# Turning 128 x 128 blocks in one run instead of one by one between other products, and new begin times for every lane of the plan

## The chip, the cores and the metric

The kernel runs on one core of a Trainium2 chip. The metric is the device time of one execution in microseconds (us), from the first to the last instruction and a little around them; the times stand below. A core has four engines that matter here: TensorE (PE, with PEld for its weight loads), VectorE (DVE), ScalarE (ACT) and GpSimd (POOL), and SyncE (SP), which here only issues the transfers.

## The reference, cut to what matters

Two models of two layers each run one after the other on 256 tokens of width 1024, all in float32.

```
for l in range(2):                                     # first model
    h += 0.5 * swiglu(rmsnorm(h), gate, up, down)      # ffn1, width 2816
    z = rmsnorm(h) @ w_in                              # mix1: latent attention (8 heads),
    h += (sum of 3 gated branches) @ w_out             #   differential attention (8 heads), pooling
    h += 0.5 * swiglu(...)                             # ffn2
h = rmsnorm(h)                                         # final
for l in range(2):                                     # second model
    x += 0.5 * rmsnorm(swiglu(rmsnorm(x)))             # ffn1_2
    x += rmsnorm(token_mixing(rmsnorm(x)))             # mix2: windowed attention, mLSTM, RWKV-7
    x += 0.5 * rmsnorm(swiglu(...))                    # ffn2_2
    x += rmsnorm(sigmoid(rmsnorm(x) @ w_gate) * (p[l] @ w_proj))   # ple
```

## The kernel before, in words

The 256 tokens are two tiles (i = 0, 1) of 128 rows. A stage is a part of a layer (`ffn1`, `mix1`, `ffn2`, `final`, `ffn1_2`, `mix2`, `ffn2_2`, `ple`); `s` counts them. The weights come from memory as one stream of pieces of 512 KB. ACT rounds each to fp32r (`whi`, L471), DVE makes the rest (`wlo`, L478), and each product of the reference is three products in fp32r (`products`, all recorded at L489): whi with the activation's high part, wlo with the high part, whi with the low part. They are called dense products here; nearly all have 512 columns.

Everything else on PE is small and in float32. There are the turns (transposes, `turns`, L498), which bring activations into the layout that the next dense products need: the normed rows (`pe_norm`, names `xs`), the hidden layer of an FFN (`pe_hidden`, names `hid`, four turns in each of 11 steps `q`), the attention weights (`pe_values1`, `pe_values2`, names `S`), the projections (`pe_chunks`), the attention outputs (`pe_turn`). Then the scores (L1411, L1420, L2401), the products with the values (L1456, L2424), the 64 x 64 products of the RWKV part (`quad`, L2050, and L2094 to L2180), and the small products of the mLSTM part (L2516 to L2553).

The order of the instructions of each engine is fixed when the program is made. Each piece of work is a generator, a lane (`pe_ffn`, `act_norm`, `dve_jobs1`, ...). A lane yields a beat, a planned time, ahead of its next instructions; `by_beat` always takes the lane with the lowest beat. A beat is only a key to sort by: on the chip, an engine runs its list in order and waits on semaphores. `timed` replaces the beats of a lane by those of the table `PLAN` for the two stages that meet (`org(s)` plus the entry); a tuple that a lane yields, as `(t + MM * q,)`, is a beat relative to its last begin time, with `MM = 0.227`. So a lane that yields such a tuple between two instructions lets other lanes put theirs in between:

```
    def gemm(...):   # dense: one beat for each product
                if q:
                    yield (t + MM * q,)
                m = pe.do.matmul(...)
    def turns(t, *each):   # turns: one beat for each
            if q:
                yield (t + MM * q,)
            m = pe.do.transpose(o, src, ident)
```

The pieces of weights are placed on ACT and DVE by `round_beat`, from the beats at which PE takes a piece and frees its slot.

Of the kernel before, what the change touches and what calls it, by code (L numbers as in the profile page):

```python
# [88 lines left out]
def by_beat(*lanes):  # L89
# [6 lines left out]
    while heads:  # L96
# [5 lines left out]
        else:  # L102
# [6 lines left out]
MM = 0.227  # L109
# [3 lines left out]
        "act_norm": (-10.4, 2.5, 2.72, 21.46),  # L113
        "act_square": (-68.48, -48, 17.2, 28.38),
        "dve_norm": (-87.72, -87.72, -70, 30.08),
        "dve_square": (16.08, 24.78),
        "pe_norm": (-171.14, -161.94, -122.64, -103.54),
        "pool_norm": (-115.96, -48.5),
    },
    "ffn1>mix1": {  # L120
        "act_back1": (72.74, 77.9, 95.8, 107.48, 125.74, 125.74, 128.12, 130.52, 135.62, 139.32, 139.4, 143.98, 148,
            158.54, 162.44, 165.88, 165.88, 168.4, 174.62, 178.06),
        "act_bias1": (-33.68,),
        "act_branch1": (128.68, 130.56, 138.26, 143.04, 160.14, 161.8, 174.62, 178.68, 187.66, 187.7, 208.74,
            208.74),
        "act_jobs1": (56.56, 66.82, 66.82, 69.38, 70.48, 81.86, 94.32, 94.32, 94.32, 99.16, 117.22, 126.44, 129,
            131.22, 131.46, 136.5, 137.28, 141.96, 146.98, 148.52, 164.4, 164.74, 168.26, 172.98),
        "act_latent": (29.56, 30.88, 31.94, 38.5, 41.42, 42.62, 42.62, 44.34, 46.06, 46.84, 49.64, 51.5, 51.94),
        "act_merged1": (199.54, 202.84, 212.96, 214.02),
        "act_norm": (16.38, 19.78, 23.28, 27.08),  # L130
        "act_pool1": (111.82, 120.26, 125.26, 145.8),
        "act_project1": (41.96, 63.54, 80.82, 105.12),
        "act_square": (23.3, 24.76, 25.46, 25.46),
        "act_sums1": (147.86, 178.34),
        "act_turn1": (113.76, 125.12, 183.62, 186.62),
        "act_turns1": (67.06, 82.3, 109.2),
        "dve_add": (11.18, 11.7, 18.62, 19.74),
# [8 lines left out]
        "dve_latent": (29.62, 29.72, 37.48, 37.66, 37.66, 37.66, 37.72, 42.96, 42.96, 42.96, 48.88, 48.88, 48.88,  # L146
            48.88, 49.82),
        "dve_merged1": (204.68, 206.66, 210.52, 217.04),
        "dve_norm": (16.44, 20.2, 24.26, 24.74),
        "dve_pool1": (104.96, 111.76, 114.08, 114.62, 117.6, 118.56, 118.56, 121.36, 122, 122.82, 123.3, 153.34),  # L150
        "dve_project1": (-13.52, 38.58, 59.42, 80.16, 100.6),
        "dve_square": (24.64, 28.44),
# [22 lines left out]
        "pool_latent": (-147.18, -147.18, -147.18, -33.98),  # L175
        "pool_norm": (-158.5, -150.14),
        "pool_sums1": (39.62, 51.14),
        "tables_in": (-1.82,),
    },
    "ffn1_2>mix2": {  # L180
        "act_front2": (43.32, 47.58, 49.7, 56.72, 78.44),
        "act_group": (141.54, 171.88),
        "act_jobs2": (130.14, 132.52, 133.06, 133.06, 134.02, 134.14, 134.14, 141.84, 144.9, 150.54, 150.78, 151.06,
            153.7, 153.96, 154.82, 164.96),
        "act_memory": (135.76, 145.1, 145.66, 150.78, 160.48, 162.82, 165.86, 172.4, 172.52, 180.96),
        "act_norm": (14.86, 20.98, 25.02, 25.02),
        "act_post": (8.6, 8.78, 8.9, 19.5),
        "act_project2": (28.12, 42.6, 53.34, 57.6, 65.86, 80.76, 99.02, 106.66, 111.42, 113.18, 148.8, 152.98),
        "act_rope2": (126.04,),
        "act_square": (17.88, 22.92, 22.92, 22.98),  # L190
# [4 lines left out]
        "dve_group": (137.5, 137.62, 161.52, 172.04),  # L195
        "dve_jobs2": (122.52, 127.36, 129.54, 136.48, 141.48, 157.3, 158.32, 162.5),
        "dve_memory": (98.1, 105.1, 107.6, 121.36, 142.68, 160.92, 161.32, 161.6, 166.22, 167.06, 167.06, 167.06,
            168.94, 169.92, 173.68, 177.28, 178.62, 179.42, 181.14),
        "dve_norm": (15.88, 22.5, 28.5, 30.52),
        "dve_post": (11.22, 13.28, 14.66, 14.66, 18.7, 18.7),  # L200
        "dve_project2": (29.88, 41.36, 41.36, 43.98, 45.34, 46.5, 51.92, 53.54, 56.7, 57.3, 59.1, 66.58, 89.12,
            152.32, 154.28),
        "dve_rope2": (109.24, 110.16, 117.32, 120.22),
        "dve_square": (23.42, 31.86),
        "dve_state": (114.28, 132.28, 134.92),
        "dve_sums2": (141.12, 150.7, 167.3, 169.66),
        "dve_turn2": (170.56, 170.56),
        "dve_unit0": (60.08, 60.52, 76.66, 83.5, 83.9, 94.78, 106.5, 111.5),
        "dve_unit1": (66.8, 75.24, 83.18, 89.18, 94.1, 99.96, 118.68, 129.28),
        "pe_front2": (45.76, 46.8, 47.38, 57.42, 58.38),  # L210
        "pe_group": (130.5, 134.34),
        "pe_memory": (130.5, 144.52, 152.86, 152.86, 159.9, 159.9, 167.26, 170.56, 174.12, 174.22, 175.88, 176.78,
            180.58),
        "pe_norm": (16.46, 20.38, 23.48, 23.48),
        "pe_out2": (177.16, 177.68, 179.46, 180.6, 180.6, 180.6, 180.6, 181.7, 184.44, 188, 188.5, 188.5, 188.58,
# [116 lines left out]
def program(nc, order, known, dram, out, vecs, consts, misc, bcs, pos, x_in):  # L332
# [861 lines left out]
    QT_BANKS = (2, 3, 4, 5, 6)  # L1194
# [1869 lines left out]
```

## Time and profile before

| | |
|---|---|
| three runs | 2436.68, 2437.96, 2438.85 us; median 2437.96 us |
| the profiled execution's own time | 2437.84 us |
| its span, first to last instruction | 2436.5 us |
| mean granted TensorE clock | 0.982 |
| PE busy | 2380.6 us, 98% of the span |
| DVE, ACT, POOL busy | 62%, 51%, 2% |
| read from memory | 396.86 MB, DMA engines busy 49.9% |

Busy times of PE overlap: a matmul's record goes from its start to its modelled end, and the next has started by then. What a product costs is therefore read from the distance between starts, not from its length. The clock column says how much of full speed the throttle granted: 1.00 is 2.4 GHz, 0.50 is 1.2 GHz.

### The profile page before, as it was taken

What the parts mean: (1) busy time and instruction counts of PE and PEld (TensorE: products, weight loads), DVE (VectorE), ACT (ScalarE), POOL (GpSimd) and SP (SyncE); (2) the same over time, 40 slices, a digit from 0 to 9 for tenths busy, and PEclk for the clock granted to TensorE, in tenths of its full rate; (3) what the DMA queues carried; (4) which work ended last, traced back from release to release, by engine and by line L of the source; (5) the groups of instructions that cost most, each with busy time, mean ns of one, the idle gap of its engine ahead of it and who ended that gap; (6) DMA issues with size and microseconds to landing.
All of it is one profiled execution on the core that took longest, in us unless ns stands there. A gap on an engine that the chain in (4) does not pass through costs nothing.

```text
span 2436.5 us, 31092 instructions
## 1 busy us (share of the span) xinstructions
PE 2380.6 (98%) x12448; PEld 1932.5 (79%) x12448; DVE 1520.9 (62%) x2296; ACT 1241.0 (51%) x2057; POOL 51.5 (2%) x66
## 2 busy tenths in 40 slices
PE   8999999999999999999999999999999999999998
PEld 6788878888888877888878878778877887877886
DVE  5656786655655778665565576665556558576555
ACT  5455554544544655454454463654455446365445
POOL 0000000000000000000000000000000000000000
PEclk9999999999999999999999999799999999979999
DMA  7555446555555434555555542155545553215563
GB/s 249 183 193 161 122 139 193 182 187 182 182 183 197 151 124 145 185 182 193 187 173 181 192 137 81 47 186 195 189 156 184 188 183 120 89 66 185 181 198 118
DMA packets 110737, 399.95 MB, mean 164 GB/s; under 512 B 12288, under 2 KB 12672, under 8 KB 110336
## 3 DMA queue, kind: packets, MB, share of 16 engines
q1 hardware_dynamic: 110592, 397.96, 49.9%
q8 instruction: 98, 1.61, 0.3%
q14 instruction: 47, 0.39, 0.0%
HBM read 396.86 MB, written 1.05 MB: 163 GB/s over the span
## 4 chain that ended last, share of the span: by engine, by line
PE 92%; DVE 4%; ACT 2%; issue 0%; POOL 0%; DMA 0%; SPq 0%; ACTq 0%
PE ps L489 81%; PE ps L498 4%; DVE wlo L478 1%; PE ps L2050 1%; PE ps L1456 1%; DVE alo L632 1%; PE ps L1420 1%; PE ps L2424 1%; ACT whi L471 0%; ACT ahi L613 0%; PE ps L1411 0%; PE ps L2553 0%; DVE xs L893 0%; PE ps L2542 0%; PE ps L2534 0%
## 5 line engine op out<-in xcount | busy, mean ns | idle before, releaser
L478 DVE TENSOR_TENSOR wlo<-raw,whi 128x1024 fp32r<-128x1024 f32 (+1 forms) x748 | 893.5, 1212 | 250.8 <-ACT whi L471 245.5
L471 ACT CAST whi<-raw 128x1024 fp32r<-128x1024 f32 (+1 forms) x748 | 764.1, 1041 | 295.1 <-PE ps L489 286.2
L489 PE MATMUL ps<-whi,ahi 128*128 128x512 f32 (+2 forms) x2016 | 812.3, 403 | 24.8 <-DVE wlo L478 18.2
L489 PE MATMUL ps<-wlo,ahi 128*128 128x512 f32 (+2 forms) x2016 | 809.4, 401 | 0.0
L489 PE MATMUL ps<-whi,alo 128*128 128x512 f32 (+2 forms) x2016 | 804.5, 399 | 0.0
L489 PEld LDWEIGHTS ps<-whi,ahi 128*128 128x128 f32 x2016 | 380.6, 189 | 124.2 <-DVE wlo L478 32.3
L489 PEld LDWEIGHTS ps<-wlo,ahi 128*128 128x128 f32 x2016 | 381.3, 189 | 82.9 <-issue 1.0
L489 PEld LDWEIGHTS ps<-whi,alo 128*128 128x128 f32 x2016 | 380.8, 189 | 81.1 <-issue 1.4
L489 PE MATMUL ps<-whi,yhi 128*128 128x512 f32 (+1 forms) x948 | 375.6, 396 | 0.5
L489 PE MATMUL ps<-wlo,yhi 128*128 128x512 f32 (+1 forms) x948 | 372.5, 393 | 0.0
L489 PE MATMUL ps<-whi,ylo 128*128 128x512 f32 (+1 forms) x948 | 372.1, 392 | 0.0
L809 DVE SCALAR_TENSOR_TENSOR hid<-ps,stat,sil 128x256 f32<-128x256 f32 x176 | 85.1, 484 | 265.8 <-ACT sil L788 265.8
L788 ACT ACTIVATE sil<-ps,stat 128x256 f32<-128x256 f32 x176 | 83.6, 475 | 327.1 <-PE ps L489 318.2
L489 PEld LDWEIGHTS ps<-whi,yhi 128*128 128x128 f32 x948 | 179.3, 189 | 38.9 <-issue 2.1
L489 PEld LDWEIGHTS ps<-wlo,yhi 128*128 128x128 f32 x948 | 179.3, 189 | 36.9 <-issue 0.7
L489 PEld LDWEIGHTS ps<-whi,ylo 128*128 128x128 f32 x948 | 178.9, 189 | 37.3
L814 DVE TENSOR_TENSOR ylo<-ps,yhi 128x512 fp32r<-128x512 f32 x88 | 60.8, 691 | 157.1 <-ACT yhi L795 156.5
L795 ACT CAST yhi<-ps 128x512 fp32r<-128x512 f32 x88 | 51.6, 586 | 210.5 <-PE ps L498 210.5
L498 PE MATMUL ps<-cst,hid 128*128 128x128 f32 x352 | 94.8, 271 | 0.0
L613 ACT ACTIVATE ahi<-ps,vec 128x128 fp32r<-128x128 f32 x224 | 62.7, 386 | 43.1 <-PE ps L498 42.8
L632 DVE SCALAR_TENSOR_TENSOR alo<-ps,vec,ahi 128x128 fp32r<-128x128 f32 x224 | 62.3, 344 | 27.2 <-ACT ahi L613 27.0
L1473 ACT ACTIVATE S<-S,sm 128x128 f32<-128x128 f32 (+1 forms) x96 | 42.9, 448 | 43.1 <-DVE sm L1504 43.0
(374 smaller groups left out, 1627.6 us busy)
## 6 DMA issues: line engine op xcount, KB each, us to landing
raw<-stream SPq DMA_DIRECT2D x718, 512.0 KB, 4.1
raw<-stream SPq DMA_DIRECT2D x16, 388.0 KB, 3.1
bcb<-bcs SPq DMA_DIRECT2D x9, 512.0 KB, 4.6
raw<-stream SPq DMA_DIRECT2D x8, 416.0 KB, 3.8
raw<-stream SPq DMA_DIRECT2D x4, 384.0 KB, 3.0
cst<-consts SPq DMA_DIRECT2D x1, 1260.0 KB, 8.1
msc<-misc SPq DMA_DIRECT2D x1, 1160.0 KB, 6.9
xs<-xin SPq DMA_DIRECT2D x2, 512.0 KB, 4.5
```

Of the source, the lines that this page charges most:

```text
L471: act.do.copy(whi[:, n % NSP, 0:w], raw[:, n % NRAW, 0:w]).then_inc(*rounded(n))
L478: dve.do.tensor_tensor(wlo[:, n % NSP, 0:w], raw[:, n % NRAW, 0:w], whi[:, n % NSP, 0:w].bitcast(F), ALU.subtract).then_inc(*rest(n))
L489: m = pe.do.matmul(o, a, b, start=(first and q == 0), stop=(last and q == n - 1))
L498: m = pe.do.transpose(o, src, ident)
L613: act.do.mul(ahi[:, c, 128 * i:128 * i + 128], ps[:, 2 * i + hf, 128 * (c % 4):128 * (c % 4) + 128], vc(GAIN[part], l, c)).then_inc(*a_hi( ...
L632: dve.do.scalar_tensor_tensor(alo[:, c, t], ps[:, 2 * i + hf, 128 * (c % 4):128 * (c % 4) + 128], vc(GAIN[part], l, c), ahi[:, c, t].bitca ...
L788: act.do.activation(sil[:, n % 4, :], ps[:, n % 3, 0:256], ACT.Silu, scale=stat[:, 6 + i:7 + i]).then_inc(*silu(s, n))
L795: act.do.copy(yhi[:, y:y + 2, :], ps[:, 3, :].rearrange("p (k t) -> p k t", k=2)).then_inc(*h_hi(s, q))
L809: dve.do.scalar_tensor_tensor(hid[:, n % 4, :], ps[:, n % 3, 256:512], stat[:, 6 + i:7 + i], sil[:, n % 4, :], ALU.mult, ALU.mult).then_in ...
L814: dve.do.tensor_tensor(ylo[:, y:y + 2, :], ps[:, 3, :].rearrange("p (k t) -> p k t", k=2), yhi[:, y:y + 2, :].bitcast(F), ALU.subtract).th ...
L1420: m = pe.do.matmul(ps[:, 5 + q, 0:k], dq[p0:p0 + 32, x // 2, n1:n1 + 128], dk[p0:p0 + 32, x // 2, 0:k], start=True, stop=True, tile_positi ...
L1473: act.do.activation(a[:, q, :], a[:, q, :], ACT.Exp, bias=sm[:, h:h + 1], accum_out=sm[:, z + h:z + h + 1]).then_inc(*job_act(s, n, "exp", q))
```

## The change

`turns` is no longer a generator: it issues all its transposes at once, so nothing can come between them. Its nine callers call it plainly, and so do the three callers of `pe_turn`. `gemm` is not touched, so the dense products still yield a beat each. Every table of `PLAN` is replaced, for PE, ACT, DVE and POOL. The core of it (entries of `PLAN` are begin times of one lane, in the order in which the lane yields them):

```
-    def turns(t, *each):
-
-        for q, (o, src) in enumerate(each):
-            if q:
-                yield (t + MM * q,)
+    def turns(*each):
+
+        for o, src in each:
             m = pe.do.transpose(o, src, ident)
         return m
...
-            m = yield from turns(0, *((ps[:, 3, 256 * k + 128 * i:256 * k + 128 * i + 128],
+            m = turns(*((ps[:, 3, 256 * k + 128 * i:256 * k + 128 * i + 128],
                                        hid[:, (2 * q + i) % 4, 128 * k:128 * k + 128]) for k in range(2) for i in range(2)))
...
     "ffn1>mix1": {
-        "pe_scores1": (55.98, 56.72, 57.12, 59.6, 61.54, 74, 78.24, 78.46, 81.96, 84.06, 97.46, 110.14, 127.1,
-            129.44, 130.18, 135.4, 137.16, 137.44, 142.34, 143.68, 149.16, 160.32, 162.96, 168.84),
+        "pe_scores1": (51.08, 55.06, 55.14, 60.54, 64.48, 69.82, 74.7, 76.14, 81.38, 87.04, 93.96, 108, 124.06,
+            127.72, 131.56, 133.5, 136.46, 141.12, 143.02, 147.36, 150.52, 152.72, 158.48, 159.4),
...
     "ffn1_2>mix2": {
-        "pe_group": (130.5, 134.34),
-        "pe_memory": (130.5, 144.52, 152.86, 152.86, 159.9, 159.9, 167.26, 170.56, 174.12, 174.22, 175.88, 176.78,
-            180.58),
-        "pe_out2": (177.16, 177.68, 179.46, 180.6, 180.6, 180.6, 180.6, 181.7, 184.44, 188, 188.5, 188.5, 188.58,
-            191.08, 196.82, 199.06, 201.24, 201.96),
-        "pe_project2": (22.1, 25.32, 26.06, 27.14, 32.48, 32.56, 39.38, 39.38, 42.66, 44.46, 44.88, 44.88, 49.86,
-            54.4, 54.4, 56.08, 66.62, 69.42, 76.2, 84.48, 94.32, 94.74, 94.74, 102.32, 112.72, 118.18, 126.16,
-            137.4),
-        "pe_scores2": (121.48, 122.78, 126.9, 128.78, 135.82, 138.08, 149.7, 157.26),
-        "pe_values2": (126.68, 127.84, 128.16, 129.78, 129.78, 135.8, 137.66, 143.1, 144.26, 156.52, 156.52, 158.9,
-            166.38, 172.64, 173.14, 174.14),
+        "pe_group": (130.7, 132.92),
+        "pe_memory": (130.74, 141.38, 148.12, 148.12, 153.14, 157.42, 165.32, 170.84, 172.12, 174.66, 178.24,
+            178.46, 182.28),
+        "pe_out2": (179.68, 179.82, 180.8, 180.82, 181.58, 181.58, 181.58, 181.58, 184.08, 184.08, 184.08, 184.98,
+            185.08, 191.66, 197.3, 198.56, 198.7, 198.7),
+        "pe_project2": (23.88, 26.3, 28.96, 29.66, 30.58, 31.66, 32.7, 32.7, 33.62, 35, 37.44, 38.16, 38.5, 39.16,
+            41.12, 43.82, 54.7, 59.3, 71.16, 80.88, 93.1, 93.9, 96.48, 107.36, 114.82, 120.82, 124.32, 137.92),
+        "pe_scores2": (118.54, 122.26, 124.28, 125.74, 131.08, 140.6, 144.06, 155.74),
+        "pe_values2": (123.72, 124.5, 124.5, 126.84, 129.4, 133.68, 136.4, 136.58, 141.44, 157.92, 162.76, 165.6,
+            166, 167.76, 167.76, 172.14),
...
     "ple>ffn1_2": {
-        "pe_norm": (13.48, 14.34, 15.5, 16.04),
+        "pe_norm": (9.78, 9.78, 23.94, 24.92),
```

The other tables change in the same manner. In `pe_values2` the entries with even number (from 0) begin the turns of attention job n, the odd ones its products with the values; the last four entries of `pe_project2` are the last dense pieces of the mLSTM projection, and `pe_out2` is the output projection.

## Rows read from the trace of the kernel before

**Rows 1.** The page: busy time of PE, and the clock in 40 slices.
```profile
PE 2380.6 (98%) x12448; PEld 1932.5 (79%) x12448; DVE 1520.9 (62%) x2296; ACT 1241.0 (51%) x2057; POOL 51.5 (2%) x66
...
PEclk9999999999999999999999999799999999979999
```

**Rows 2.** Waits of PE: who waited for whom, us in total, times, longest.
```profile
PE ps L489 <- DVE wlo L478: 18.2, 17, 3.2
PE ps L498 <- DVE xs L893: 6.8, 6, 3.4
PE ps L498 <- DMA vec<-vecs: 5.5, 1, 5.5
...
PE ps L1456 <- ACT PT L1484: 0.7, 2, 0.4
...
PE ps L498 <- ACT S L2436: 0.2, 1, 0.2
```

**Rows 3.** Timeline of PE, an FFN step: start us, length us, instruction.
```profile
57.55 0.40 PE L489 MATMUL ps<-whi,ahi 128*128 128x512 f32 x1
57.79 0.27 PE L498 MATMUL ps<-cst,hid 128*128 128x128 f32 x1
...
58.14 0.27 PE L498 MATMUL ps<-cst,hid 128*128 128x128 f32 x1
...
59.40 0.39 PE L489 MATMUL ps<-whi,ahi 128*128 128x512 f32 x1
```

**Rows 4.** The chain that ended last, one piece: start us, us, what.
```profile
59.10 15.66 PE ps L489 x69
```

**Rows 5.** Timeline of PE: first and last turn that stands alone between dense products.
```profile
28.83 0.27 PE L498 MATMUL ps<-cst,hid 128*128 128x128 f32 x1
...
2400.24 0.40 PE L498 MATMUL ps<-cst,xs 128*128 128x128 f32 x1
```

**Rows 6.** Timeline of PE, mix2: four turns in one run between dense products.
```profile
1466.72 0.40 PE L489 MATMUL ps<-whi,ahi 128*128 128x512 f32 x1
1466.96 0.40 PE L489 MATMUL ps<-wlo,ahi 128*128 128x512 f32 x1
1467.19 0.60 PE L1953 MATMUL ps<-cst,up 128*128 128x128 f32 x4
...
1467.87 0.27 PE L2077 MATMUL ps<-cst,B__119 128*128 128x128 f32 x1
```

**Rows 7.** Timeline of PE, mix2: 64 x 64 products between dense ones of 388 columns.
```profile
1471.95 0.34 PE L489 MATMUL ps<-whi,alo 128*128 128x388 f32 x1
1472.13 0.34 PE L489 MATMUL ps<-whi,ahi 128*128 128x388 f32 x1
1472.40 0.68 PE L2050 MATMUL ps<-um 64*64 64x64 f32 x16
1473.01 0.45 PE L489 MATMUL ps<-wlo,ahi 128*128 128x388 f32 x1
1473.29 0.34 PE L489 MATMUL ps<-whi,alo 128*128 128x388 f32 x1
```

**Rows 8.** Windows of 10 us: busy PE, PEld, DVE, ACT, POOL; granted clock; DMA.
```profile
1530.00:1540.00 10.00, 8.93 (x63) 5.58 (x60) 7.55 (x19) 7.56 (x20) 0.00 (x0) 1.00 0.19 55
1540.00:1550.00 10.00, 7.77 (x39) 5.76 (x38) 9.55 (x17) 9.90 (x18) 0.00 (x0) 0.86 0.00 1
1550.00:1560.00 10.00, 10.00 (x32) 6.68 (x32) 6.08 (x13) 7.13 (x18) 0.00 (x0) 0.50 0.01 2
```

**Rows 9.** Timeline of PE: the dense products around two stretches without any.
```profile
1531.30 0.40 PE L489 MATMUL ps<-whi,alo 128*128 128x512 f32 x1
...
1537.76 0.50 PE L489 MATMUL ps<-whi,ahi 128*128 128x512 f32 x1
...
1541.46 0.39 PE L489 MATMUL ps<-whi,alo 128*128 128x512 f32 x1
...
1574.69 0.77 PE L489 MATMUL ps<-whi,yhi 128*128 128x512 f32 x1
```

More of the change, by code:

```diff
@@ L112 @@
     ">ffn1": {
[L113 to L118, printed above, removed]
+        "act_norm": (15.74, 16.72, 19.22, 27.56),
+        "act_square": (-20.64, -11.94, 14.36, 19.12),
+        "dve_norm": (15.62, 23.28, 25.3, 29.06),
+        "dve_square": (11.18, 27.42),
+        "pe_norm": (-26.56, -26.38, -21.98, -16.42),
@@ L119 @@
+        "pool_norm": (-17.96, 6.36),
     },
     "ffn1>mix1": {
[L121 to L127, printed above, removed]
@@ new lines @@
+        "act_norm": (16.52, 19.84, 23.28, 23.4),
+        "act_pool1": (103, 106.88, 114.72, 128.44),
+        "act_project1": (54.04, 67.8, 80.58, 94.78),
+        "act_square": (15.86, 19.54, 23.96, 26.82),
+        "act_sums1": (146.06, 181.52),
+        "act_turn1": (103.2, 105.62, 182.2, 183.26),
+        "act_turns1": (59.58, 88.32, 99.52),
+        "dve_add": (12.96, 17.58, 18.26, 20.48),
[7 rows of a table added]
+        "dve_latent": (30.22, 30.22, 31.82, 32.96, 34.68, 35.16, 37.98, 39.94, 39.94, 39.94, 40.06, 44.38, 44.38,
+            46.16, 50.52),
@@ L263 @@
-        "pool_norm": (-60, 14.66),
-        "pool_post": (-99.14, -67.56),
+        "act_norm": (12.74, 13.94, 18.62, 19.56),
+        "act_ple": (29.32, 34.34, 35.16, 41.02),
+        "act_post": (10.38, 10.38, 12.7, 17.06),
+        "act_square": (21.6, 21.68, 21.68, 21.96),
+        "dve_norm": (15.52, 15.52, 19.66, 21.74),
+        "dve_ple": (32.98, 33.94, 36.08, 44.1),
+        "dve_post": (8.08, 8.08, 8.08, 14.94, 17.74, 18.1),
+        "dve_square": (29.76, 31.06),
+        "pe_norm": (15.66, 15.88, 20.3, 20.3),
@@ L309 @@
+        "act_post": (6.56, 9.38, 15.58, 19.26),
+        "act_square": (18.96, 19.72, 24.22, 27.24),
+        "dve_norm": (18.02, 23.52, 23.52, 26.58),
+        "dve_post": (9.28, 10.54, 12.96, 13.34, 19.14, 19.14),
+        "dve_square": (26.58, 28.46),
+        "pe_norm": (9.78, 9.78, 23.94, 24.92),
+        "pool_norm": (15.98, 44.74),
+        "pool_post": (-30.86, 8.8),
     },
@@ L595, in pe_norm @@
                 wait_banks(s, i, hf)
-                m = yield from turns(0, *((ps[:, 2 * i + hf, 128 * c:128 * c + 128],
+                m = turns(*((ps[:, 2 * i + hf, 128 * c:128 * c + 128],
                                            xs[:, i, 512 * hf + 128 * c:512 * hf + 128 * c + 128]) for c in range(4)))
@@ L976, in pe_turn @@
     def pe_turn(sig, s, name, o, bank, b):
-        m = yield from turns(0, *((ps[:, bank, 256 * c + 128 * i:256 * c + 128 * i + 128],
+        m = turns(*((ps[:, bank, 256 * c + 128 * i:256 * c + 128 * i + 128],
                                    o[:, i, 256 * b + 128 * c:256 * b + 128 * c + 128]) for c in range(2) for i in range(2)))
@@ L1034, in pe_chunks @@
                 yield (4 * MM,)
-            m = yield from turns(4 * MM * b, *((ps[:, banks[b], 256 * c + 128 * i:256 * c + 128 * i + 128],
+            m = turns(*((ps[:, banks[b], 256 * c + 128 * i:256 * c + 128 * i + 128],
                                                   src(i)[:, 256 * b + 128 * c:256 * b + 128 * c + 128])
@@ L1202, in pe_latent @@
             pe.wait_ge(front_dve, s, "cn", 1, g)
-            m = yield from turns(4 * MM * g, *((ps[:, 2 + g, 256 * (c % 2) + 128 * i:256 * (c % 2) + 128 * i + 128],
+            m = turns(*((ps[:, 2 + g, 256 * (c % 2) + 128 * i:256 * (c % 2) + 128 * i + 128],
                                                   cn[:, i, 128 * c:128 * c + 128]) for c in cs for i in range(2)))
@@ L1248, in pe_latent @@
                 pe.wait_ge(front_dve, s, "v", 0)
-            m = yield from turns(0, *((ps[0:96, QT_BANKS[b], 256 * (h % 2) + 128 * i:256 * (h % 2) + 128 * i + 128],
+            m = turns(*((ps[0:96, QT_BANKS[b], 256 * (h % 2) + 128 * i:256 * (h % 2) + 128 * i + 128],
                                        qs[:, i, h, :]) for h in ((2 * b, 2 * b + 1) if b < 4 else (8,)) for i in range(2)))
@@ L1437, in pe_values1 @@
                 pe.wait_ge(job_dve, s, n, "mix")
-            m = yield from turns(0, *((ps[:, 7, 128 * j:128 * j + 128], a[:, 128 * j:128 * j + 128])
+            m = turns(*((ps[:, 7, 128 * j:128 * j + 128], a[:, 128 * j:128 * j + 128])
                                       for j in range(2 * (i + 1) if kind == "mla" else i + 1)))
@@ L1588, in pe_turn1 @@
                     pe.wait_ge(*back_turn1(s, 7))
-                yield from pe_turn(job_pe, s, kind, o, bank[b], b)
+                pe_turn(job_pe, s, kind, o, bank[b], b)
     def act_turn1(s, l):
@@ L2384, in pe_rope2 @@
             pe.wait_ge(rec_dve, s, 1, "T")
-            m = yield from turns(0, *((ps[:, 4 + b, 256 * (c % 2) + 128 * i:256 * (c % 2) + 128 * i + 128],
+            m = turns(*((ps[:, 4 + b, 256 * (c % 2) + 128 * i:256 * (c % 2) + 128 * i + 128],
                                        qk2[:, i, 2 * c:2 * c + 2, :].rearrange("p h d -> p (h d)"))
@@ L2413, in pe_values2 @@
                 pe.wait_ge(lstm_dve, s, "mq")
-            m = yield from turns(0, *((ps[:, 7, 128 * q:128 * q + 128], S2[:, n % 2, 128 * q:128 * q + 128])
+            m = turns(*((ps[:, 7, 128 * q:128 * q + 128], S2[:, n % 2, 128 * q:128 * q + 128])
                                       for q in range(2 * (i + 1))))
@@ L2489, in pe_turn2 @@
             pe.wait_ge(job_dve, s, "out", 1)
-            yield from pe_turn(job_pe, s, "att", o_att, 5 + b, b)
+            pe_turn(job_pe, s, "att", o_att, 5 + b, b)
     def act_turn2(s):
@@ L2556, in pe_memory @@
         pe.wait_ge(lstm_dve, s, "out", 1)
-        yield from pe_turn(lstm_pe, s, "mem", hm, 0, 0)
+        pe_turn(lstm_pe, s, "mem", hm, 0, 0)
     def act_memory(s, l):
```

219 lines of the change are left out of this document (101 added, 118 removed), and 57 rows, old and new, of the table PLAN.

## The prediction

> **What bounds the kernel now.** I read the page first: PE is busy 98% of the span, and its clock is at full speed but for two slices with a 7 in them [rows 1]. So PE is the bound, and three things can change the time: how long PE's list takes back to back, how long it waits, and how long its clock is low. The waits of PE come next: 15 rows with 46.7 us in all, from 18.2 us for the low parts of the weights down to 0.2 us [rows 2]. Of these about 9 us belong to the start (5.5 us for the first transfer [rows 2], then 3.2 us for the first low part, the longest of its row). Some 38 us of waits are left that an order could remove or add to, 1.6% of the span. Third, the timeline shows how PE's list is spaced. In an FFN, 69 dense products take 15.66 us, 0.227 us each [rows 4], and where a turn stands between two of them the spacing widens [rows 3]. Last, the windows give the clock: it fell to 0.50 some 7 us after the last dense product at 1541.46 and stayed low till the output projection began at 1574.69 [rows 8, 9]; the second layer does the same around 2149 to 2184. Those two stretches take about 65 us, half of it lost to the clock.
>
> **The turns in one run.** In the FFN step of [rows 3] four turns stand singly. From the dense product at 57.55 to the one at 59.40 are 1.85 us with six dense products in them; 1.85 - 6 x 0.227 = 0.49 us for four turns, 0.12 each. The nearest case of four in one run is in mix2 [rows 6]: from 1466.72 to 1467.87 are 1.15 us with three dense products and four turns. With 0.227 a product the turns take 0.47 us; with the 0.24 that the two dense starts there stand apart, 0.43. So a run of four saves between 0.02 and 0.06 us; I take 0.04. Over the whole timeline of PE, 636 turns stand alone between dense products, the first at 28.83 and the last at 2400.24 [rows 5], which is 159 runs of four: 159 x 0.04 = 6.4 us, bounds 3.2 and 9.5. 3.5 us of it lies in the FFNs (88 steps, eight stages of 11), where PE never waits and the saving goes straight to the end.
>
> A rule speaks against the change. The Trainium skill, "TensorE: Matmul & The Clock Gate", part 2 on issuing a matmul, says that the next weights load while the current product still runs. Taken alone it would make a single turn nearly free (its 128-column load lies behind a 512-column product) and a run of turns bound by its loads. By that page's gap of about 56 ns for 128 columns, an estimate, four single turns would cost 0.22 us, and the change would lose. The trace does not agree: four single turns cost 0.49 us [rows 3], a little more than four in a run [rows 6]. The sum goes by the rows.
>
> **Fewer runs of small products.** The planner's count of changes should show in how often small work interrupts the dense products. I sorted the begin times of the table, old and new, with 0.227 between dense products. By the old table a mix1 layer has 52 interruptions that hold a product other than a turn, a mix2 layer 25, the same numbers that the timeline shows. By the new one they are 44 and 22: 22 fewer over the four layers. An interruption by 64 x 64 products costs its own work and the two ends: 0.27 us from dense to the first of them, where 0.18 is the spacing of 388 columns, and 0.28 for the dense product behind them [rows 7], so 0.09 + 0.10 = 0.19 us. For full-height products beside turns the ends may cost nothing. So 22 x 0 to 0.19 = 0 to 4 us; I take 2, since most of the removed ones are scores and value products of the attention.
>
> **The waits.** ACT, DVE and POOL get new orders too, and their work is the same. Where they are off the path, that costs nothing; it is hidden behind PE, which is busy 98%. Where they aren't, the 38 us can go either way. The new order joins things that depend on each other. In `pe_values2` the turns of job 3 begin at 136.4 and its value product at 136.58, those of job 6 at 166 and 167.76 with nothing of PE between; the value product needs ACT's copy of the turned block. Where this happens now PE waits 0.35 us (0.7 us in 2 times, L1456 [rows 2]). It also puts the last scores and turns of one run behind a wait of DVE. On the other side the table for `ple>ffn1_2` moves the turns of tile 1 behind the first dense products (23.94 where 15.5 was), which now hold the FFN up: PE waits 6.8 us for `xs` (L893) in all [rows 2]. What is late next there is DVE, which owes the low parts of both activation and weights. I take zero for the sum of waits, with -12 and +12 as bounds, a third of 38 us each way.
>
> **The sum.** The profiled execution's own time is 2437.84 us, 1.3 above its span and 0.1 from the median. 6.4 + 2 + 0 = 8.4 us less: 2429.5 us, 0.35% faster. What a measurement of this kernel can tell from no change is about 0.2%, 4.9 us: faster ends at 2433.1, slower begins at 2442.8.
>
> **The rivals.**
> - *The likeliest (0.43):* as summed, 2429; its own range 2423 to 2435.
> - *The waits shrink too (0.17).* The boundary waits for `wlo` and `xs` are 25 us, 3.2 at the start [rows 2]. If the new begin times take half of the rest, 11 us, the time is 2418. For it: each wait of over 3 us between stages is followed by some us at the low clock, which would go as well. Against: there DVE and ACT are busy nearly all the time, so a new order only moves their debt.
> - *The gain is given back (0.24).* Pairs set next to each other as above, 0.35 to 0.8 us each, twice a layer in mix2, and similar pairs in the 24 attention jobs of mix1; with about 7 us of new waits the time is 2436, no change that can be told.
> - *The clock falls earlier in mix2 (0.12), the one on the other side.* Today 6.46 us without a dense product (1531.30 to 1537.76) leave the clock at 1.00 [rows 8, 9]. The new table puts nine begin times in that place (126.8 to 136.6, from `pe_values2` 3 to 7, `pe_group`, `pe_memory` 0 and `pe_scores2` 4), with the value product of job 3 behind its own turns, and only then the last 12 dense products. The work of it is about 5 us and its waits 1.5, so it is as long as today's. If a longer wait in it brings the low clock there, then the 12 dense products (2.7 us more), the first 7 us of the stretch behind them less their 2 us of waits (5 us more) and 1 to 2 us of the run itself go at half speed: 9 us a layer, 18 in two. 2429 + 18 = 2447. It decides from the point where the clock's row of that run shows less than 1.00. The Trainium skill says on the page named above, in its part on transposes, that transposes don't count as activity for the clock; the trace agrees in so far as PE was busy 10.00 of 10 us with small work at a clock of 0.50 [rows 8].
> - *Runs of turns are bound by their loads (0.04),* the page's rule above. As a mechanism of this kernel: if the four in a run of [rows 6] were cheap only by the place, and cost 0.12 more than singly, the change loses 159 x 0.12 = 19 us less 2: 2455.
>
> **How the numbers follow.** Faster by over 0.2%: nearly all of the first and second, 0.60. Within: the third and the edge of the first, 0.25. Slower: the last two, less a little, 0.15. The range reaches from half of the second case to the bound where slower begins: 2415 to 2443. It leaves out the far part of the second case and most of the last two, under 2 in 10.
>
> **What would show each step.** In an FFN, the timeline shows four turns as one row `x4`, and the distance of the dense products around it is 0.45 us more than their own time, not 0.49. No turn stands alone. The waits of PE stay between 35 and 58 us in all. The interruptions in mix2 are 22 and in mix1 44. The clock shows two stretches at 0.50 of some 30 us each, beginning behind the last dense product of `pe_project2`; if they begin before it, the fourth case holds. The prediction fails if the total of the waits moves by over 10 us, or a third long stretch at 0.50 comes up, or one goes.

## The result and the profile after

The changed kernel takes 2422.38 us (median of 4 runs, 2420.52 to 2422.64), the kernel before 2438.4 us beside it (4 runs, 2436.68 to 2439.02). The ratio is 0.9934, interval 0.9917 to 0.9951: about 16 us or 0.66% faster. The forecast was 8.4 us less; the gain is nearly twice that.

The page of the changed kernel, busy time and clock:

```profile
PE 2369.2 (98%) x12448; PEld 1941.0 (80%) x12448; DVE 1517.8 (63%) x2296; ACT 1238.3 (51%) x2053; POOL 48.3 (2%) x66
...
PEclk9999999999999999999999999799999999979999
```

PE has as many instructions as before and is busy 11.4 us less [rows 1], with the same two slices at 7. The idle time of PE fell by another 4.2 us; the two make the 15.6 us between the spans of the two profiled executions (2436.5 and 2420.9). Its waits: engine and line, what it waited for, us in total, times, longest.

```profile
PE ps L487 <- DVE wlo L476: 14.0, 11, 3.0
PE ps L487 <- DVE alo L628: 11.1, 5, 3.9
PE ps L494 <- DMA vec<-vecs: 4.7, 1, 4.7
PE ps L2420 <- ACT PT L2441: 2.4, 4, 0.7
PE ps L494 <- DVE xs L889: 2.0, 3, 1.3
```

Against [rows 2], the waits for `wlo` and `xs` shrank (18.2 to 14.0, 6.8 to 2.0), and two grew: `alo` (11.1 us; the row of the kernel before stands below) and, as the prediction feared, the value product set right behind its own turns (2.4 us in 4 times). All 14 rows add up to 42.3 us where 46.7 were.

```profile
PE ps L489 <- DVE alo L632: 3.9, 3, 3.4
```

The FFN step, timeline of PE in the changed kernel (start, length, instruction), which answers to [rows 3]:

```profile
57.11 0.39 PE L487 MATMUL ps<-whi,ahi 128*128 128x512 f32 x1
57.34 0.60 PE L494 MATMUL ps<-cst,hid 128*128 128x128 f32 x4
57.70 0.48 PE L487 MATMUL ps<-wlo,ahi 128*128 128x512 f32 x1
58.01 0.39 PE L487 MATMUL ps<-whi,alo 128*128 128x512 f32 x1
```

The four turns are one row x4. From 57.11 to 58.01 is 0.90 us for two dense products and four turns: 0.90 - 2 x 0.227 = 0.45 us, which looks as forecast. It isn't: over six products, as [rows 3] was read, the turns cost 0.48 us in the mean of 56 steps (e1 below). In order of start, the 636 turns that stood alone between dense products are now 156 runs of four, and four turns alone.

The first stretch at the low clock, in windows as [rows 8] (window, length, busy PE, PEld, DVE, ACT, POOL, clock, DMA):

```profile
1530.00:1540.00 10.00, 8.78 (x49) 5.96 (x49) 9.02 (x22) 9.88 (x16) 0.00 (x0) 0.99 0.00 1
1540.00:1550.00 10.00, 9.32 (x36) 7.33 (x36) 8.73 (x13) 6.64 (x18) 0.00 (x0) 0.50 0.00 0
1550.00:1560.00 10.00, 10.00 (x37) 8.08 (x37) 4.44 (x12) 4.33 (x13) 0.00 (x0) 0.50 0.01 2
1560.00:1570.00 10.00, 10.00 (x38) 9.03 (x37) 8.42 (x21) 5.16 (x10) 2.93 (x2) 0.50 0.19 56
1570.00:1580.00 10.00, 10.00 (x46) 8.22 (x46) 7.13 (x9) 4.33 (x6) 0.00 (x0) 0.98 0.86 268
```

It begins some 5 us behind the last dense product of `pe_project2` (1534.47) and ends 5 us behind the first of the output projection (1565.32).

**Two measures for all runs.** First, the distance from the last FFN step of one part to the first of the next, by the turns of `hid`. Second, the time lost to the clock: (1 - clock) x length, over the whole span. PE's idle time stands beside it, start and end included. All are of one profiled execution each, in us. (The recorded expectations leave the last 0.9 to 2.5 us of the span out and so quote 0.4 to 1.3 us less.)

| kernel | span | mix1, each | final | mix2, first / second | ple | end | lost to clock | PE idle |
|---|---|---|---|---|---|---|---|---|
| before | 2436.5 | 257.4 | 33.1 | 210.8 / 211.0 | 71.9 | 56.0 | 43.6 | 55.9 |
| after | 2420.9 | 256.5 | 30.6 | 206.3 / 207.5 | 70.5 | 54.8 | 37.8 | 51.7 |
| e1, block, old table | 2436.0 | 257.1 | 32.5 | 210.8 / 210.9 | 73.2 | 56.5 | 47.0 | 56.7 |
| e2, single, new table | 2448.9 | 262.8 | 31.5 | 212.3 / 212.3 | 71.6 | 55.2 | 39.4 | 72.3 |
| e3, new mix2 | 2436.2 | 257.2 | 32.4 | 210.7 / 210.7 | 73.5 | 56.6 | 50.4 | 57.3 |
| e8, mix2 and its exit | 2424.9 | 257.1 | 32.4 | 204.8 / 207.6 | 72.0 | 56.4 | 40.4 | 55.0 |
| e9, its complement | 2428.6 | 257.1 | 30.6 | 210.4 / 210.6 | 70.5 | 54.8 | 36.8 | 55.8 |
| e5, second model new | 2419.3 | 257.2 | 30.6 | 204.7 / 205.4 | 70.5 | 54.8 | 34.1 | 56.1 |

The 15.6 us between the spans of before and after: 8.0 in the two mix2, 2.5 in `final`, 2.5 in `ple` and the end together, 1.9 in the two mix1, 0.8 in the eight FFN stages (ten steps each, some 160 us), 0.4 at the start, less 0.4 from `ffn2` to `ffn1`.

The time lost to the clock is an upper bound of what the low clock costs. The four runs of e11 lie between 2424.10 us at a mean clock of 0.989 and 2432.41 at 0.983: 15 us more lost by this measure, 8 us more time. And 2.7 us of it before and 2.0 after lie behind PE's last product, where it costs nothing. It also differs between runs of one kernel, so that a single piece of 1.7 us in a profile says little: the five runs of e5 have mean clocks of 0.984 to 0.986, 34 to 39 us lost.

### The profile page after: what moved, and what is told of

It is laid out like the page before. It is cut to its first block, busy times and chain, and to the rows that moved or that the text cites. A ratio compares the mean times of both kernels' runs of the same rounds, so it can differ in the third digit from the quotient of the medians.

```text
span 2420.9 us, 31095 instructions
## 1 busy us (share of the span) xinstructions
PE 2369.2 (98%) x12448; PEld 1941.0 (80%) x12448; DVE 1517.8 (63%) x2296; ACT 1238.3 (51%) x2053; POOL 48.3 (2%) x66
## 3 DMA queue, kind: packets, MB, share of 16 engines
q1 hardware_dynamic: 110592, 397.96, 50.4%
q8 instruction: 98, 1.61, 0.3%
## 4 chain that ended last, share of the span: by engine, by line
PE 90%; DVE 6%; ACT 3%; issue 1%; DMA 0%; POOL 0%; SPq 0%; ACTq 0%; DVEq 0%
PE ps L487 79%; PE ps L494 4%; DVE wlo L476 2%; PE ps L2046 1%; PE ps L1452 1%; ACT whi L469 1%; PE ps L2420 1%; PE ps L1416 1%; DVE alo L628 1%; PE ps L2549 0%; ACT ahi L609 0%; PE ps L1407 0%; PE ps L2538 0%; DVE tm L2016 0%; PE ps L2530 0%
## 5 line engine op out<-in xcount | busy, mean ns | idle before, releaser
L487 PE MATMUL ps<-whi,ahi 128*128 128x512 f32 (+2 forms) x2016 | 798.2, 396 | 26.1 <-DVE wlo L476 14.0
L487 PE MATMUL ps<-wlo,ahi 128*128 128x512 f32 (+2 forms) x2016 | 795.9, 395 | 0.0
L487 PE MATMUL ps<-whi,alo 128*128 128x512 f32 (+2 forms) x2016 | 788.7, 391 | 0.0
L487 PEld LDWEIGHTS ps<-wlo,ahi 128*128 128x128 f32 x2016 | 380.3, 189 | 73.2 <-issue 3.5
L1469 ACT ACTIVATE S<-S,sm 128x128 f32<-128x128 f32 (+1 forms) x96 | 43.0, 451 | 30.6 <-DVE sm L1500 30.5
L494 PEld LDWEIGHTS ps<-cst,hid 128*128 128x128 f32 x352 | 43.9, 141 | 11.2 <-DVE hid L805 0.3
```

The source lines that it names most:

```text
L487: m = pe.do.matmul(o, a, b, start=(first and q == 0), stop=(last and q == n - 1))
L1469: act.do.activation(a[:, q, :], a[:, q, :], ACT.Exp, bias=sm[:, h:h + 1], accum_out=sm[:, z + h:z + h + 1]).then_inc(*job_act(s, n, "exp", q))
```

## The experiments

**e1: the turns in one run, nothing else.**

```diff
-    def turns(t, *each):  # a generator, 4 begin times
+    def turns(*each):
+        for o, src in each:
+            m = pe.do.transpose(o, src, ident)
+        return m
 PLAN = { ... }   # as in the kernel before
```

> The turns in one run, with every begin time of the table as before. Theory A (the prediction's term: four turns in a run save 0.04 us against four single ones, 159 times): 6.4 us less than the kernel before, 2432. Theory B (the stage lengths of the changed kernel: ten FFN steps went from 160.12 to 160.07 us, so a run saves 0.01 us): 1 to 2 us less, 2436.5 to 2437.5, no change that can be told; all the rest of the 16 us is the table's.

Measured: 2436.39 us (11 runs), before 2437.53; ratio 0.9996, interval 0.9987 to 1.0005. So the run of turns alone gives 1 us, at most 3, and by the interval perhaps nothing. The eight FFN stages are 0.8 us shorter in all, 0.01 us for each of their 80 runs where 0.04 had been forecast; 159 runs by 0.01 are 1.6 us, which agrees with the time. (In the profile other parts moved as well: `ple` is 1.3 us longer, with 1.7 us more lost to the clock, `final` 0.6 shorter.) The timeline shows which reading failed, once single turns and runs are read in the same place over the same number of products. From the dense product ahead of the turns to the sixth behind it, the mean of 56 steps (the second to the ninth of every FFN but the first) is 1.853 us before, 1.843 in e1 and 1.844 in the kernel after. Less 6 x 0.227, the four turns cost 0.49, 0.48 and 0.48 us. The other 66 products of a step take 14.98 us in all three. So the 0.49 of [rows 3] was right, and the price of a run was too low: its 0.43 to 0.47 came from another place, mix2 [rows 6]. Ten steps (683 dense products and 40 turns) tell the same: 160.12 us before and 160.08 in e1 (second FFN), which by 0.227 a product leaves 0.127 and 0.126 us a turn.

**e2: the new table with divided turns,** the other half.

```diff
 PLAN = { ... }   # as in the kernel after
     def turns(t, *each):   # as in the kernel before, and its callers
```

> The new table with the turns still divided, one beat each. Theory A: the run of turns is worth 6.4 us here too, so 2422.4 + 6.4 = 2429. Theory B: it is worth 1 to 2 us, 2424. A third, C: the new begin times were laid out for runs, and divided turns come later to those who wait for them, so that waits grow: over 2430.

Measured: 2450.32 us (5 runs), ratio 1.0054, interval 1.0041 to 1.0067: slower than both kernels. The waits of PE in e2, columns as above:

```profile
PE ps L462 <- DVE wlo L451: 28.4, 23, 3.0
PE ps L462 <- DVE alo L605: 12.4, 9, 3.9
...
PE ps L462 <- DVE ylo L1301: 3.0, 2, 1.5
```

PE is idle 72.3 us where the changed kernel has 51.7, and each mix1 takes 6.3 us more. In the first mix1, PE waits 4.9 us where it waits 0.2 in the kernel after. One of those waits is 1.61 us, ahead of the dense product at 408.80, for the low part of a weight. The two parts of the change can't be priced singly: the block alone gives about 1 us, the table alone costs 13, both together give 16.

**e3: turns in one run, and of the new table only the mixer of the second model.**

```diff
 PLAN = {
-    "ffn1_2>mix2": { ... },   # as before
+    "ffn1_2>mix2": { ... },   # as after
```

> Turns in one run, and the new begin times for the stage mix2 alone (the table for the pair ffn1_2 and mix2), all others as before. By the distances between the FFN steps on either side, the two mix2 stages gave 4.5 and 3.5 us of the gain. If that is what these tables do by themselves, this is 8 us under the run with all old begin times. If part of it comes from the tables of the neighbouring stages (the weights are placed by what PE takes there), it is less, 3 to 6 us.

Measured: 2436.53 us (11 runs), ratio 0.9995, interval 0.9986 to 1.0003. No gain, against both expectations. The stretch without a dense product ahead of the output projection did shrink, from 33.4 us in e1 to 31.0 in both mix2. What took it back lies at the two ends of the mixer: at its entry PE now waits 2.05 us for `alo`, and the clock falls behind it (at 1421 and 2025 us); at its exit the clock falls as well (at 1602 and 2206). The time lost to the clock rose by 3.4 us against e1.

**e5: turns in one run, all tables of the second model new, those of the first old.**

```diff
 PLAN = {
-    "ffn2>final", "final>ffn1_2", "ffn1_2>mix2", "mix2>ffn2_2", "ffn2_2>ple", "ple>ffn1_2", "ple>": as before
+    the same seven: as after
```

> Turns in one run, and the new begin times for everything from the end of the first model on; the first model as before. By the distances between FFN steps the second model and the passage into it hold 2.5 + 4.5 + 1.35 + 3.5 + 1.15 = 13 us of the 15.6: 13 us under the run with all old begin times, some 2424. The first model then holds 2 us at most.

Measured: 2420.95 us (5 runs), ratio 0.9935, interval 0.9921 to 0.9948: the whole gain, 3 us more than expected. What the first model's new tables do can be read between e5 and the kernel after: mix1 256.46 and 256.47 instead of 257.16 and 257.21, 1.4 us less in both; `ffn2` to `ffn1` 27.82 instead of 27.11, 0.7 more.

**e8 and e9: the second model cut once more.** e8 has the new tables of the mixer and of the change of part behind it; e9 all new tables of the second model but the mixer's. The tables differ in rows such as this:

```diff
     "mix2>ffn2_2": {
-        "dve_post": (2.18, 4.82, 4.82, 15.08, 16.8, 19.44),
+        "dve_post": (9.9, 9.9, 10.04, 16.24, 16.44, 17.94),
```

> Turns in one run, the old begin times except in two tables: that of the second model's mixer and the one behind it, with the norm between mixer and FFN. The new mixer table alone measured 0.9995, and its trace shows why it might: it makes the slow stretch 1.7 us cheaper, but TensorE then waits 2.7 us more at the exit and the clock falls a second time there (0.61, at 1600 and at 2205). Theory C (what the mixer's table brings is lost at its old exit): mixer to FFN takes 205 to 207 us twice instead of 210.8, and the kernel 2426 to 2430 us. Theory D (the gain comes from the tables of the other changes of part, and the mixer only looks shorter by it): 2434 to 2437 us.

> The complement: turns in one run, all of the second model's new tables but that of its mixer. Theory C: the exits alone cannot save the mixer's part; mixer to FFN 209 to 211 us, and only the parts between models (final to ffn1_2, -2.0), ple (-1.3) and the end (-1.1) are kept: 2430 to 2434 us. Theory D: most of the gain is here, 2422 to 2427 us, and the slow stretch (17.1 us lost to the clock in the kernel before it) is as short as in the kernel after (12 to 15.4).

Measured: e8 2428.2 us (5 runs), ratio 0.9960, interval 0.9946 to 0.9974. e9 2429.78 us (6 runs), ratio 0.9969, interval 0.9957 to 0.9980. Theory C holds (e9 a little below its range of 2430 to 2434): with the mixer's table or the exit's alone mix2 takes 210.4 to 210.8 us, with both 204.8 and 207.6. The exit of the first mix2 in windows as above, first e3 (old exit), then e8 (new exit):

```profile
1595.00:1600.00 5.00, 3.03 (x11) 1.61 (x10) 4.87 (x8) 4.91 (x8) 0.56 (x1) 1.00 0.30 91
1600.00:1605.00 5.00, 3.93 (x15) 3.32 (x16) 4.43 (x11) 2.99 (x12) 0.55 (x1) 0.66 0.82 270
```

```profile
1595.00:1600.00 5.00, 4.86 (x25) 3.58 (x24) 5.00 (x10) 5.00 (x15) 1.46 (x1) 1.00 0.71 220
1600.00:1605.00 5.00, 5.00 (x24) 4.14 (x23) 3.08 (x9) 4.36 (x6) 0.55 (x1) 1.00 0.54 189
```

And the waits of PE from 1585 to 1615 us, e3 and then e8:

```profile
PE ps L469 <- DVE xs L864: 1.9, 2, 1.5
PE ps L462 <- DVE wlo L451: 1.4, 1, 1.4
```

```profile
PE ps L462 <- DVE wlo L451: 1.3, 1, 1.3
PE ps L469 <- DVE xs L864: 0.4, 1, 0.4
```

The exit comes a few us earlier in e8, so the whole of it is to be compared: from 1590 to 1610, PE is idle 3.39 us in e3 and 1.41 in e8, and the clock falls in e3 alone (0.66 is the mean of a window in part at 0.50). The entry of the first mix2, windows as above, first e3, then e8:

```profile
1420.00:1425.00 5.00, 4.75 (x18) 4.01 (x19) 4.94 (x11) 4.39 (x13) 0.55 (x1) 0.66 0.47 159
```

```profile
1420.00:1425.00 5.00, 5.00 (x26) 3.73 (x25) 4.95 (x10) 5.00 (x17) 0.02 (x1) 1.00 0.54 153
```

Both wait 2.05 us for `alo` just ahead of it; the clock falls behind that wait in e3 and not in e8. With it the account closes. In each mix2, PE is idle 1.6 us less in e8. The clock took 1.7 us less in the second (its exit) and 5.1 less in the first (entry, stretch and exit, 1.7 each). That is 3.3 us, where the second is 3.1 shorter, and 6.7, where the first is 5.9 shorter. The entry's 1.7 is not the exit table's doing, since the second mix2 has the fall at its entry in both kernels.

Against e1, e9 brings 1.9 us in `final`, 2.7 in `ple` and 1.7 at the end.

**e6 and e7: can the low clock be kept away?** The two stretches at 0.50 hold 31 of the 37.8 us lost to the clock in the kernel after. These two kernels add products to the kernel after that nothing reads, among the small ones of the stretch.

```diff
+    def fill(o, k):
+        w = MISC["pool_w", 0]
+        for _ in range(k):
+            pe.do.matmul(o, cc("bones"), msc[:, w:w + o.shape[-1]], start=True, stop=True)
 in pe_values2, per job:
-            pe.wait_ge(job_act, s, n, "exp", 1)
             ... wait for "back" of job n - 1 ...
+            if n > 1:
+                fill(ps[:, 7, 0:256], 2)      # e7: 1
+            pe.wait_ge(job_act, s, n, "exp", 1)
             m = turns(...)
 in pe_memory, ahead of the scores of head h, and of the 128x65 products of tile i:
+            fill(ps[:, h % 2, 0:256], 1)
+            fill(ps[:, 2 + i, 0:256], 2)      # e7: 1
```

> The kernel after, with extra products that nothing reads, put among the small ones of the stretch at clock 0.50 in each mix2 (27 us of turns, 128x64, 64x256, 4x256 and 128x65 products, from 1538 to 1570 in the kernel after; 15.4 us lost to the clock by sum of (1 - clock) times time): two plain 128x256 products of constants into bank 7 ahead of the turns of six of the eight jobs of the attention, one ahead of each of the four score products of the memory, two ahead of each of the two groups of 128x65. That is 20 products of about 0.43 us at full clock, 8.6 us per mix2, some of it in time in which TensorE waits. Theory A (the clock falls because small products leave too much of the array idle though the profile shows PE busy): the clock stays at 1.00 through most of the stretch, which is then 13.5 + 8.6 = 22 us instead of 29, and the kernel takes 2410 to 2416 us. Theory B (the clock falls because of the waits just ahead, 1 to 1.7 us between 1529 and 1539, or at this place whatever runs): the clock is 0.50 as before and the extra products cost up to twice, 8.6 to 17 us per mix2: 2438 to 2456 us.

> As the kernel before it, with half as many extra products: one ahead of the turns of each of the six jobs, one ahead of each of the four score products and one ahead of each of the two groups of 128x65, 12 of about 0.43 us, 5.2 us per mix2. Theory A (the clock follows how much the array does): the share of large products in the stretch is smaller, so the clock holds in part of it only: 2412 to 2425 us. Theory B (the waits ahead of it, or the place): 2432 to 2443 us, half the loss of the kernel with twice as many.

Measured: e6 2421.58 us (4 runs), ratio 0.9934, interval 0.9921 to 0.9948; e7 2415.54 us (4 runs, up to 2421.09), ratio 0.9914, interval 0.9900 to 0.9927. The time lost to the clock fell from 37.8 to 12.0 and 10.1 us. So theory A holds for the clock; e7 lies in its range, e6 above it (2410 to 2416 had been expected) and below that of B. Against the ratio of the kernel after (0.9934, interval 0.9917 to 0.9951) e7 is about 5 us faster; the intervals overlap, though three of its four runs, 2413.7 to 2416.3, lie below all of that kernel's. The fourth, 2421.09, has a mean clock of 0.993 where the three have 0.996 and 0.997. e7 over the stretch, windows as above:

```profile
1530.00:1540.00 10.00, 9.10 (x50) 6.00 (x47) 8.27 (x17) 9.52 (x20) 0.00 (x0) 1.00 0.09 37
1540.00:1550.00 10.00, 9.73 (x53) 6.51 (x52) 8.59 (x15) 8.73 (x18) 0.00 (x0) 1.00 0.01 2
1550.00:1560.00 10.00, 8.12 (x46) 6.07 (x45) 7.49 (x19) 5.28 (x15) 0.00 (x0) 0.93 0.00 0
1560.00:1570.00 10.00, 9.16 (x51) 7.85 (x50) 8.59 (x21) 5.43 (x10) 2.93 (x2) 0.90 0.23 59
```

One piece of it in both kernels, timeline of PE; first e7, then the kernel after:

```profile
1546.72 0.65 PE L2404 MATMUL ps<-msc,cst 128*128 128x256 f32 x2
1547.21 0.60 PE L494 MATMUL ps<-cst,S 128*128 128x128 f32 x4
```

```profile
1543.98 1.06 PE L494 MATMUL ps<-cst,S 128*128 128x128 f32 x4
...
1546.12 1.97 PE L2420 MATMUL ps<-qk,PT 128*128 128x64 f32 x8
```

Four turns last 0.60 us instead of 1.06. Each added product takes about 0.5 us (it shows as two rows), so the 12 of e7 cost 6 us in each mix2 and take some 14 us off the time lost to the clock; e6 pays for 20. Part of the rest goes into waits: PE is idle 56.8 us in e7 and 51.7 in the kernel after. The Trainium skill ("TensorE: Matmul & The Clock Gate", Part 4 on the transpose) says that transposes don't count as PE being busy in the usual way; the traces agree that small work alone goes with the low clock (PE busy 10.00 of 10 us at 0.50 in the kernel after, 1550 to 1560), and e7 shows products of 256 columns among it at 1.00. But only 24 of the some 120 instructions of the stretch are turns, the others small products; no run here has turns alone.

**e10 and e11: each half of the fills.** e10 has one ahead of the turns of jobs 3 to 7, none in the memory; e11 has only the six of the memory.

```diff
 e10:  pe_values2:  if n > 2: fill(ps[:, 7, 0:256], 1)
 e11:  pe_memory:   fill(ps[:, h % 2, 0:256], 1)  and  fill(ps[:, 2 + i, 0:256], 1)
```

> The kernel after with extra products in the attention's part of the stretch alone: one plain 128x256 product of constants ahead of the turns of jobs 3 to 7, five in each mix2; one call of it takes 0.53 us at clock 1.00 in the kernel with twelve. Theory A1 (some large products anywhere among the small ones hold the clock): lost time to the clock as with twelve (9 us in all), 2.6 us of extra work instead of 5.8 per mix2, and some of it in waits: 2410 to 2414 us. Theory A2 (how much there is of them counts, part by part): the clock still falls at the memory's part and the 24 products of 128x65, so 5 to 12 us of the 26 saved are lost again: 2417 to 2426 us.

> The kernel after with the other half: one extra product ahead of each of the four score products of the memory and of each of the two groups of 128x65, none in the attention. Theory A1: 2411 to 2415 us. Theory A2: the attention's part (eight products of 128x64 and four turns per job, five jobs) falls to 0.50, and the kernel is between those with none and with twelve, 2416 to 2424 us.

Measured: e10 2419.61 us (4 runs), ratio 0.9926, interval 0.9912 to 0.9941; e11 2429.16 us (4 runs, 2424.1 to 2432.41), ratio 0.9958, interval 0.9942 to 0.9975. Lost to the clock: 29.6 and 41.1 us; the profile of e11 is of its slowest run. The traces show what theory A2 said: half the products leave the clock at 0.50 in part (e10) or nearly all (e11) of the stretch. Its range holds for e10 alone; e11 is 5 us above it, as it pays for its products nearly without a return. e11, windows as above:

```profile
1540.00:1550.00 10.00, 9.33 (x34) 5.81 (x31) 8.62 (x15) 6.63 (x11) 0.00 (x0) 0.67 0.00 0
1550.00:1560.00 10.00, 9.32 (x35) 7.11 (x34) 4.56 (x10) 5.72 (x17) 0.00 (x0) 0.50 0.01 2
```

**e12: the version that beats both.** e5 with eleven fills in each mix2 (jobs 3 to 7, four scores, two groups of 128x65).

```diff
 PLAN = { ... }   # as e5
+            if n > 2:
+                fill(ps[:, 7, 0:256], 1)
+            fill(ps[:, h % 2, 0:256], 1)
+            fill(ps[:, 2 + i, 0:256], 1)
```

> The candidate: the second model's new tables alone, turns in one run, and extra products ahead of the turns of jobs 3 to 7, of the four score products and of the two groups of 128x65: eleven in each mix2. Kernel e5 lost 33.2 us to the clock in its profile and the kernel after 37.4; with twelve fills 8.8 was left. If the two tables that e5 leaves old (0.9 us per mix1 longer, 0.7 us from FFN to FFN shorter) are the only difference to the kernel with twelve: 2415 to 2417 us; a fill less per mix2 gives back 0.5 us each: 2414 to 2416.

Measured: 2414.4 us (4 runs, 2413.06 to 2415.42), ratio 0.9904, interval 0.9890 to 0.9919: 23 us below the kernel before and 8 below the kernel after, all four runs below all of that kernel's. Its mix2 take 201.1 and 202.4 us, 6.9 us are lost to the clock in the whole span, and its clock line has no 7, as in e6 and e7:

```profile
PEclk9999999999999999999999999999999999999999
```

**e13: the same twelve fills in the kernel before.** The edit is that of e7, on the old order with divided turns.

```diff
+            if n > 1:
+                fill(ps[:, 7, 0:256], 1)
             m = yield from turns(0, ...)
+            fill(ps[:, h % 2, 0:256], 1)
+            fill(ps[:, 2 + i, 0:256], 1)
```

> The kernel before, with the twelve extra products per mix2 that brought the kernel after from 2422.4 to 2415.5 us and its time lost to the clock from 37.4 to 8.8 us. With the clock at 1.00 in the stretch in both kernels, what is left between them is what the change brings without it. Theory E (most of the change's gain is waits and order, the slow stretch is as long in both, 15.4 us lost): the extra products bring here what they brought there, 7 us, and this kernel takes 2429 to 2432 us, 14 to 16 above the one after with them. Theory F (most of the gain in the mixer was that the new order runs less of its work at the low clock): this kernel comes to 2420 to 2425 us, within 10 us of the other. If the extra products delay a chain that the old order has on its path, neither holds: 2434 or more.

Measured: 2440.8 us (12 runs), ratio 1.0024, interval 1.0012 to 1.0035: neither E nor F. The runs fall into two groups, seven of 2437.9 to 2441.1 and five of 2448.9 to 2451.4; the profile is of one of the latter. The mean clock is 0.987 to 0.989 in the seven and 0.981 to 0.984 in the five, 0.981 to 0.983 in the kernel before. So in the seven the fills did win clock, 12 to 17 us by the measure above, and the time was still 2 to 3 us longer: their own work, some 12 us, is as much. In the five they won 5 us of clock at most. The stretch of the profiled run, windows as above:

```profile
1540.00:1550.00 10.00, 8.54 (x47) 6.20 (x43) 9.09 (x18) 9.88 (x18) 0.00 (x0) 0.94 0.00 1
1550.00:1560.00 10.00, 10.00 (x30) 6.63 (x30) 6.80 (x13) 5.29 (x10) 0.00 (x0) 0.50 0.01 2
1560.00:1570.00 10.00, 10.00 (x30) 6.67 (x29) 2.07 (x7) 3.75 (x11) 0.00 (x0) 0.50 0.00 0
```

Here the clock fell in spite of the fills, from 1549 to 1586 us, and the first mix2 takes 218.9 us. So theory A of e6 is not the whole account. What differs ahead of the fall is idle time. Waits of PE from 1530 to 1550 in e13, then from 1530 to 1545 in e7:

```profile
PE ps L2317 <- DVE B__119 L2336: 1.1, 1, 1.1
PE ps L2401 <- DVE S L2464: 0.8, 1, 0.8
PE ps L2408 <- ACT og L1873: 0.7, 1, 0.7
```

```profile
PE ps L2427 <- ACT PT L2448: 0.5, 1, 0.5
PE ps L2313 <- DVE B__119 L2332: 0.4, 1, 0.4
PE ps L2404 <- ACT og L1869: 0.2, 1, 0.2
```

2.6 us in 20 us against 1.1 (e7 has no further wait up to 1550). That the new order's shorter waits are what lets the fills work is argued from these rows and not shown; no run took those waits alone away. e12 speaks against their sum as the measure: behind 1549 it waits 0.7, 0.5 and 0.7 us within 9 us, at full clock:

```profile
1550.00:1560.00 10.00, 8.79 (x55) 6.87 (x55) 7.21 (x21) 6.71 (x19) 0.00 (x0) 1.00 0.00 0
```

## Why the prediction was right, and where it was not

- **That it is faster,** and that PE is the bound throughout, held. The time lies in the range (2415 to 2443), 7 us below the predicted one. That it does is in good part luck: the largest term of the sum brought a sixth of what it was to bring, the second can't be shown, and the gain came from places where the sum had nothing.
- **The turns in one run, 6.4 us: the term that failed.** e1 measured about 1 us, where 3.2 was the lower bound. The step was the price of a run, "0.47 us" and "0.43", read in mix2: in the FFN a run costs 0.48 and four single turns 0.49, so 0.01 us is saved and not 0.04. The rule weighed there (single turns free, runs bound by loads) doesn't hold here either: single turns cost 0.12 us each, and as a rival it was to cost 19 us.
- **Fewer interruptions, 2 us: the count was right, the price isn't shown.** In order of start, work other than turns stands between dense products 44 times in each mix1 and 22 times in each mix2, as read off the table (52 and 26 before, not 25). The mix1 tables bring 0.7 us each (e5 against the kernel after), but 0.45 of that is idle time of PE. What is left, 0.25 us for eight interruptions less, is 0.03 each, against the forecast's 0.09.
- **The waits, 0 between -12 and 12.** The sum stayed in the stated 35 to 58 us: 42.3. But zero was the wrong middle. By the PE idle time 4.2 us went. The wait for `xs` on which the prediction built fell from 6.8 to 2.0, the `wlo` one by 4.2, and `alo` took 7.2 of it back: the debt of DVE did move, as the second rival's counterargument has it, but not all of it.
- **The clock was no term of the sum, and it was the second one missing.** 43.6 us lost before, 37.8 after. Of the difference 0.7 lies behind PE's last product; the other 5.1 are the most that this can have brought. Before, the clock also fell for a moment at about 1230, 1795 and 2400 us (1.7 us lost each time), each time behind a wait of PE of 1.8 to 3.4 us; the kernel after has none of these three and a new one at 2014 (1.7), behind a wait of 2.05. The same wait at the entry of the first mix2 has none behind it. The long stretch of the second mix2 lost 1.7 us less. The prediction named this ("each wait of over 3 us between stages is followed by some us at the low clock") in the second rival alone. Of its two ingredients, at most 9.3 us came: the outcome lies between the likeliest and that rival (2418).
- **The rivals.** The pairs in mix2 exist and cost what was said (0.53 us at 1531.38, 0.68 at 1549.62), 2.4 us in all, but weren't enough to give the gain back. The earlier fall in mix2 didn't come: the twelve dense products end at 1534.47 at full clock. (The clock had fallen 5.7 us behind the last dense product before, not 7, and falls 5.3 us behind it after.) The loads don't bound a run.
- **The size.** Turns 1 us, the tables of the two mix1 1.4, waits and clock outside mix1 at most 8.4. The two mix2 hold half of the gain, 8.0 us, and there these measures don't reach: PE is idle 2.2 us less, and the time lost to the clock is the same, 32.5 us in both kernels. 4.5 of the 8.0 us lie in the two stretches without a dense product ahead of the output projection (33.2 and 33.5 us before, 30.9 and 31.4 after), with as many instructions in them. Taken singly, e8 and e9 bring 8 and 7 us against e1, together nearly the 15 of e5; only the mixer's table and its exit's don't add up, which alone bring 0.1 to 0.4 us in a mix2 and together 3 to 6.

Three things stay open: where 5.8 of the 8.0 us of the two mix2 come from, since neither waits nor the clock hold them; why the mixer's table and its exit's need each other (the windows show where the time goes, not which begin time does it); and what decided between the two groups of e13.

## What to carry to other kernels

When PE is busy 98% and an order is laid out anew, don't stop at the price of the instructions that changed neighbours; look at the idle time ahead of each place where the clock falls, for it costs the wait and may cost up to 1.7 us more behind it, as at four places here. A difference of two prices below 0.05 us is worth nothing when they come from two places; read both in the same place, over many steps. And test a new order with its new blocks: the table without them lost 13 us, though both together won 16.

## What the hardware showed that was not expected

- With PE shown busy 10.00 of 10 us the clock stood at 0.50 over turns and products of 64 and 65 columns; twelve added products of 128x256, some 6 us of work, held it at 0.90 to 1.00 over the same work and made the kernel 5 to 7 us faster (e7; 5 by the ratios, 7 by the medians). Six in one half of the stretch, without the others, made it 6 to 7 us slower (e11).
- The same twelve products in the old order didn't bring the fallen clock back for 37 us in the profiled run (e13, 1549 to 1586). In e7, where it fell at 1559, it was back at 1562, 3 us ahead of the output projection.
- Four turns of 128x128 cost 0.49 us when each stands alone between dense products of 512 columns, and 0.48 us in one run: joining them brings 0.01 us per run.
- The same wait of PE of 2.05 us is followed by a fall of the clock in some places and executions and not in others (at the entry of the first mix2: in e3 and e7, not in e8 and the kernel after).
